# The recurrent heads of a two-block transformer: reordered engine queues, and the masked copy ahead of the operands' update at each level

## What is computed

```
def hgrn2_mixer(q_raw, f_raw, i_in, g_raw, lb, onorm_w):
    """S_t = diag(f_t) S_{t-1} + (1 - f_t) outer i_t ; o_t = S_t^T q_t ; chunkwise."""
    ...
    o = o * lax.rsqrt(jnp.mean(o * o, axis=-1, keepdims=True) + EPS)
    o = o * onorm_w.astype(f32).reshape(HG_HEADS, HG_DV)
    o = o.reshape(bsz, L, HG_WIDTH) * jax.nn.silu(g_raw.astype(f32))

def conv_module(u, cv_w, cv_b, ln_w, ln_b):
    """GLU -> causal depthwise conv over positions -> LayerNorm over channels -> swish."""
    ...
        o_a = hgrn2_mixer(hq, hf, hi, hg, lower_bounds[l], hg_onorm_w[l])
        o_b = dsa_mixer(sq, sk, sv, iq, ik, iw)
        o_c = conv_module(cu, cv_w[l], cv_b[l], cv_ln_w[l], cv_ln_b[l])
        mix = jnp.concatenate([o_a, o_b, o_c], axis=-1) @ w_out[l]
        x = x + g1 * mix
```

## Time and profile before

| | |
|---|---|
| median of 3 runs | 1258.82 us (1256.19 to 1261.29) |
| profiled execution: its time, its span | 1258.17 us, 1256.4 us |
| TensorE busy | 1204.6 us, 96% of the span |
| VectorE, ScalarE, GpSimd busy | 803.6, 689.9, 430.2 us |
| TensorE's granted clock, mean | 0.986 |
| windows of the heads, about | 698 to 866 us from the span's start |

### The profile page before, as it was taken

One profiled execution on the slowest core, in us unless ns is written; L12 is line 12 of the kernel. 1 busy time (PEld: TensorE's weight loads), 2 busy tenths in 40 slices (PEclk: granted clock), 3 DMA queues, 4 the chain that ended last, 5 costly groups with the idle time before them and its releaser, 6 DMA issues. The chain is left out here.

```text
span 1256.4 us, 19744 instructions
## 1 busy us (share of the span) xinstructions
PE 1204.6 (96%) x7198; PEld 976.2 (78%) x7198; DVE 803.6 (64%) x1695; ACT 689.9 (55%) x1337; POOL 430.2 (34%) x260
## 2 busy tenths in 40 slices
PE   9999999997999999999999898788899999999998
PEld 8777777775887777788676676566888889889897
DVE  6776667774577677665798666565763257365575
ACT  6766666674346776735667776533432254353443
...
DMA packets 37983, 127.62 MB, mean 102 GB/s; under 512 B 4592, under 2 KB 7280, under 8 KB 37888
## 3 DMA queue, kind: packets, MB, share of 16 engines
...
q10 hardware_dynamic: 2528, 4.98, 1.2%
...
## 5 line engine op out<-in xcount | busy, mean ns | idle before, releaser
L612 POOL TENSOR_TENSOR wL<-w,wH 128x1024 fp32r<-128x1024 f32 x89 | 222.6, 2505 | 721.6 <-ACT wH L2252 721.4
L1047 PE MATMUL G<-hi,wH 128*128 128x512 f32 x1032 | 421.0, 408 | 13.6 <-DVE xT L1142 9.5
L1049 PE MATMUL G<-hi,wL 128*128 128x512 f32 x1032 | 405.6, 393 | 0.0
L1048 PE MATMUL G<-lo,wH 128*128 128x512 f32 x1032 | 405.5, 393 | 0.0
L1047 PEld LDWEIGHTS G<-hi,wH 128*128 128x128 f32 x1032 | 195.5, 189 | 64.0 <-issue 20.3
L1049 PEld LDWEIGHTS G<-hi,wL 128*128 128x128 f32 x1032 | 195.4, 189 | 43.0
L1048 PEld LDWEIGHTS G<-lo,wH 128*128 128x128 f32 x1032 | 195.8, 190 | 38.9 <-issue 1.9
L2252 ACT ACTIVATE wH<-w 128x1024 fp32r<-128x1024 f32 x140 | 147.5, 1055 | 110.2 <-PE G L1049 59.6
L2805 DVE TENSOR_TENSOR wL<-w,wH 128x1024 fp32r<-128x1024 f32 x51 | 62.2, 1221 | 11.1 <-ACT wH L2252 10.3
L1164 DVE CUSTOM_DVE_ANT_0 adaw<-adaw,scr 128x1024 f32<-128x1024 f32 x36 | 62.9, 1747 | 0.0
L1202 ACT ACTIVATE scr<-scr,sa 128x256 f32<-128x256 f32 (+2 forms) x64 | 35.2, 557 | 23.7 <-DVE sa L1189 23.7
...
## 6 DMA issues: line engine op xcount, KB each, us to landing
...
```

The lines of the kernel that those rows point to most:

```text
L612: g.tensor_tensor(wL[:, u.slot], raw_home(u), wH[:, u.slot].bitcast(f32), ALU.subtract).then_inc(w_lo, 1)
L1047: mm(home[:, :], whi, H[:, k, :], start=(k == first), stop=False)
L1048: mm(home[:, :], whi, L[:, k, :], start=False, stop=False)
L1049: last = mm(home[:, :], wlo, H[:, k, :], start=False, stop=(k == final))
```

## The change

Nothing is computed otherwise. `level_of` runs `joined` and then `raise_both`, where it was the other way about. On VectorE `clamped` and `powers` move from the end of a window and from behind `queries_1` to the window's start, and `silu_vector_2` behind `raise_q`; the norm of the head before stands behind level 3 in place of level 2, its gate behind level 4 and its low part behind level 5; the logistic steps stand later too. On ScalarE the terms, splits and logistic steps are in another order; window 1 takes eight pairs of terms and window 2 three. TensorE begins head 1's first unit before window 0, and in the last window fewer tiles stand ahead of `outputs(3)` and more behind it. Four of the blocks of the modulation go from `add_output` to the end of the last head on VectorE, and their loads move ahead in SyncE's queue.

```diff
-CONV_HEAD = [4, 7, 4, 0]
+CONV_HEAD = [4, 8, 3, 0]
...
-ADA_PER = {"a": (ADA_OA, (0, 1, 1, 1, 1, 0, 0, 0), 32), "b": (ADA_OB, (0, 1, 1, 1, 1, 2), 32), "m": (ADA_OM, (0, 1, 1, 1, 1, 2), 48)}
+ADA_PER = {"a": (ADA_OA, (0, 0, 0, 1, 1, 1, 1, 0), 32), "b": (ADA_OB, (0, 1, 1, 1, 1, 2), 32), "m": (ADA_OM + 4, (0, 0, 0, 1, 1, 0), 48)}
...
-            for n in range(4):
+            for n in range(5):
                 load_unit(Unit(UOM + 1 + n))
-            for n in range(8):
+            for b in range(2, 6):
+                load_ada(Block(ADA_OM, b))
+            for n in range(1, 8):
                 load_unit(Unit(UOM + 5 + n))
-                if 1 <= n <= 4:
-                    load_ada(Block(ADA_OM, n + 1))
             load_ada(Block(ADA_M, 0))
...
+            conv_terms(0, 0)
+            split_h(4)
+            conv_terms(0, 1)
+            conv_terms(0, 2)
+            conv_terms(0, 3)
+            split_h(5)
+            for t in range(1, 4):
+                split_h(4 * t + 2)
+                for slot in range(6):
+                    conv_terms(t, slot)
+                split_h(4 * t + 3)
                 split_h(4 * t + 4)
-                conv_terms(t, 4 if t else 3)
+                conv_terms(t, 6)
+                conv_terms(t, 7)
                 if t < 3:
                     split_h(4 * t + 5)
-                conv_terms(t, 5)
-                conv_terms(t, 6)
...
-            v.memset(stat[:, b.buffer, 0, 0:1], 0.0)
+            v.memset(stat[:, b.buffer, 1, 0:1], 0.0)
...
+                gemm_h(1, 0, (2,))
                 product(0, 0)
                 product(0, 1)
-                gemm_h(1, 0, (0, 1))
+                gemm_h(1, 0, (3, 4))
                 product(0, 2)
                 turn_h(0)
-                gemm_h(1, 0, (2, 3, 4))
+                gemm_h(1, 0, (5,))
                 product(0, 3)
-                gemm_h(1, 0, (5, 6, 7))
+                gemm_h(1, 0, (6, 7))
                 product(0, 4)
...
                 sum_h(t - 1)
+
+            def window(t):
+
+                opened(t)
                 fill(t, 3)
                 product(t, 3)
-
-            def window(t):
-
...
+                if t == 2:
+                    conv_sum()
                 fill(t, 4)
...
-                    conv_sum()
                 fill(t, 5)
                 product(t, 5)
...
                 fill(t, 6)
                 product(t, 6)
-                if t == 2:
-                    conv_sqsum()
                 fill(t, 7, (0, 1))
                 product(t, 7)
...
                 opened(3)
+                fill(3, 3, (0, 1))
+                product(3, 3)
+                fill(3, 3, (2, 3))
+                product(3, 4)
                 output_m(0, (4, 5))
-                output_m(0, (0,))
-                product(3, 4)
-                output_m(0, (1,))
+                product(3, 5)
                 output_m(1, (4, 5))
-                product(3, 5)
+                product(3, 6)
+                output_m(0, (0, 1))
+                product(3, 7)
                 output_m(1, (0, 1))
-                output_m(0, (6,))
-                product(3, 6)
-                output_m(0, (7,))
+                turn_ke(3)
+                output_m(0, (6, 7))
+                updates(3)
                 output_m(1, (6, 7))
-                product(3, 7)
-                output_m(2, (4, 5, 6))
-                turn_ke(3)
-                output_m(2, (7, 0))
-                output_m(0, (2,))
-                updates(3)
-                output_m(1, (2,))
-                output_m(2, (1,))
                 outputs(3)
-                output_m(2, (2,))
-                output_m(3, (4, 5))
+                output_m(2, (4, 5))
                 sum_h(3)
-                output_m(3, (6, 7, 0, 1, 2))
+                for n in range(2):
+                    output_m(n, (2,))
+                output_m(2, (6, 7, 0, 1, 2))
+                output_m(3, (4, 5, 6, 7, 0, 1, 2))
...
             turn_c(pe, 4)
-            gemm_h(0, 3, SECOND)
+            gemm_h(0, 3, (4, 5))
             mix_c(pe, 4)
+            gemm_h(0, 3, (6,))
             turn_c(pe, 5)
+            gemm_h(0, 3, (7,))
+            gemm_h(1, 0, (0,))
             mix_c(pe, 5)
+            gemm_h(1, 0, (1,))
             spread_c(pe, 0)
...
+                terms(CONV_C[5], CONV_C[6])
+                take_hv(0)
+                gate_1(0)
                 conv_terms(0, 0)
-                take_hv(0)
-                conv_terms(0, 1)
-                gate_1(0)
-                conv_terms(0, 2)
                 split_h(4)
                 forget(1)
                 silu_scalar_2(act, "h", 0, zsig)
-                conv_terms(0, 3)
+                conv_terms(0, 1)
+                conv_terms(0, 2)
                 keys(1)
                 factor(1)
+                take_first(0)
+                conv_terms(0, 3)
                 split_h(5)
-                take_first(0)
...
             def window(t):
-                queries(t)
+                raw_h(t, 1, qraw, sem("h_q"), t + since("h_q"))
                 take_ke(t - 1)
+                act.wait_ge(sem("h_raw1"), t + 1 + since("h_raw1"))
+                silu_scalar_1(act, link, "hq", t, qraw[:, :], kraw[:, :])
+                split_h(4 * t + 2)
+                silu_scalar_2(act, "hq", t, kraw[:, :])
                 conv_terms(t, 0)
-                silu_scalar_2(act, "hq", t, kraw[:, :])
-                split_h(4 * t + 2)
                 raw_h(t, 2, vraw, sem("h_vturn"), t + since("h_vturn"))
+                if t == 3:
+                    for k in range(2):
+                        act.wait_ge(sem("conv_z"), k + 1)
+                        silu_scalar_1(act, link, "cv", k, cacc[:, k, :], cv_th[k])
                 conv_terms(t, 1)
+                square_h(t - 1)
+                conv_terms(t, 2)
                 if t == 3:
                     for k in range(2):
                         silu_scalar_2(act, "cv", k, cv_th[k])
-                square_h(t - 1)
-                split_h(4 * t + 3)
-                conv_terms(t, 2)
-                take_hv(t)
-                root_h(t - 1)
-                if t == 3:
                     for k in range(2):
                         act.wait_ge(sem("cv_gated"), k + 1)
                         s.activation(hi1[:, 6 + k, :], cv_th[k], ACT.Copy).then_inc(sem("cv_gated_hi"), 1)
                 conv_terms(t, 3)
+                take_hv(t)
+                root_h(t - 1)
+                conv_terms(t, 4)
                 raw_h(t, 3, zraw, sem("h_silu"), t + since("h_silu"))
-                split_h(4 * t + 4)
                 gate_1(t)
-                conv_terms(t, 4)
-                gated_h(t - 1)
-                if t < 3:
-                    split_h(4 * t + 5)
+                conv_terms(t, 5)
+                split_h(4 * t + 3)
                 if t == 2:
                     for k in range(2):
                         act.wait_ge(sem("conv_centred"), k + 1)
                         s.activation(csq[:, k, :], cacc[:, k, :], ACT.Square).then_inc(sem("conv_sq"), 1)
-                conv_terms(t, 5)
+                gated_h(t - 1)
+                if t < 3:
+                    forget(t + 1)
+                    split_h(4 * t + 4)
                 silu_scalar_2(act, "h", t, zsig)
                 conv_terms(t, 6)
-                if t < 3:
-                    forget(t + 1)
                 if t == 2:
                     act.wait_ge(sem("conv_sqsum"), 1)
                     rsqrt_scalar(link, 1, 1.0 / 256, sem("conv_var"), sem("conv_root"))
                 if t < 3:
                     keys(t + 1)
                     factor(t + 1)
-                if t == 2:
-                    for k in range(2):
-                        act.wait_ge(sem("conv_z"), k + 1)
-                        silu_scalar_1(act, link, "cv", k, cacc[:, k, :], cv_th[k])
                 take_first(t)
+                conv_terms(t, 7)
+                split_h(4 * t + (5 if t < 3 else 4))
 
...
             def level_of(t, n):
+                joined(t, n)
                 raise_both(t, n)
-                joined(t, n)
...
+                level_of(0, 2)
                 low_c(dve, 0)
-                level_of(0, 2)
+                level_of(0, 3)
                 low_c(dve, 1)
-                level_of(0, 3)
                 level_of(0, 4)
+                level_of(0, 5)
                 silu_vector_1(dve, "h", 0, zraw[:, :], zsig)
                 gates(1)
-                level_of(0, 5)
                 level_of(0, 6)
-                clamped(1)
                 raise_both(0, 7)
+            def conv_root():
+                dve.wait_ge(sem("conv_root"), 1)
+                rsqrt_vector(link, 1)
+
+            def conv_scaled(k):
+                w0, b1 = VEC["cv_ln_w_2"], VEC["cv_ln_b_2"]
+                link(v.scalar_tensor_tensor(out=cacc[:, k, :], in0=cacc[:, k, :], scalar=vecT[:, w0 + k:w0 + k + 1],
```

(44 more changed lines are left out.)

30 lines of the change are left out of this document (8 added, 22 removed).

## The result

| | before | changed |
|---|---|---|
| median | 1259.99 us (1256.19 to 1261.29) | 1215.11 us (1214.12 to 1215.96, 4 runs) |
| ratio, 95% interval | 1 | 0.9648 (0.9624 to 0.9673) |
| profiled execution: time, span | 1258.17, 1256.4 us | 1215.79, 1214.0 us |
| mean granted clock | 0.986 | 0.997 |

The account below looks back on a forecast made before the run. TensorE, busy 96% of the span, was taken as the bound, so only its waits and slow stretches could be won: 22.9 + 6.0 − 0.5 − 2.0 = 26.4 us off 1258.2, so 1232 us, range 1223 to 1245.

Parts of the forecast that it names:

- the idle time that this change can reach: TensorE's waits before window 0, in windows 0 to 3 and two behind window 3: 31.3 us in sum.
- the floor of 38.8 us: Most that could be won: 31.3 us of TensorE's idle time plus 7.5 us of slow clock, with no matmul taken away.
- the price of the slow stretches: TensorE's lower clock around five waits, estimated at 1.5 us each, 7.5 in all; four were to go, saving 6.0.
- The waits of the heads: TensorE's waits left before window 0, in windows 0 to 3 and the tail: 8.4 us of 31.3, so 22.9 saved.
- half of one: VectorE operations with two SBUF inputs beside GpSimd: half the 1.2 us stretch counted, giving window 1 a 1.0 us wait.
- Window 3's mechanism: Product 5 waits 3.0 us for level 4, behind ScalarE's root and the norm, with only two tiles per level.
- The tail's two waits: Behind window 3, 3.6 us each for the last head's low part and for rms: both go, 0.5 left.
- the 2.0 kept back: 2.0 us taken off the gain for waits missed in a count by tenths and for a second slow stretch.
- the 0.5 for short pieces: An estimated 0.5 us taken off the gain for more and shorter pieces between TensorE's products.
- the raise becomes the wait: Rival 1: products wait for VectorE's copy, raise and stretched operations, mainly windows 0 and 1; 1240 to 1242 us; chance 0.17.
- The wait did not move into window 3: Rival 2: root, norm and level 4 come later than counted, waits return in window 3; price 15, 1247 us; chance 0.09.
- no load of a block reached TensorE: Rival 4: the load for the block ahead of `states_of(3)` comes late, VectorE and TensorE stand; slower, 1265 us; chance 0.04.

Follow-up runs that it names:

- a_only: The kernel before with only the table of modulation blocks at the first attention's output units changed: 1247.42 us, ratio 0.9899.
- a_back: The changed kernel with only the table of the first output's blocks put back as before: 1226.63 us, ratio 0.9745 to the kernel before.
- norm_back: The changed kernel with the norm of the head before behind level 2 again, not level 3: 1216.28 us, ratio 0.9665 to the kernel before.
- raise_first: The changed kernel with the raise ahead of the masked copy within a level, as before: 1212.44 us, ratio 0.9632 to the kernel before.

## Why the prediction was wrong

**The step that failed** is the first part's "the idle time that this change can reach is 1.7 + 3.9 + 4.9 + 3.3 + 10.3 + 3.6 + 3.6 = 31.3 us", and with it the floor of 38.8 us, "no more": 42.4 were won. The sum has no term for the table of the first output's blocks. It is in the diff, and TensorE's longest wait of the whole span belonged to it. It measured 11.6 us (**a_only**), 11.5 undone (**a_back**). With it the same sum would have given 1220. A second term was too small as well, the price of the slow stretches: 7.5 us for the five that it counted, where the trace shows some 10.2 (below).

**The waits of the heads were right in the sum**, 8.4 us left forecast and 8.5 measured:

| | forecast | measured |
|---|---|---|
| before window 0 | 0.2 | 0 |
| window 0 | 1.8 | 0.91 |
| window 1 | 1.0 | 0.63 + 2.56 |
| window 2 | 1.2 | 0.56 |
| window 3 | 3.7 | 1.90 + 0.33 |
| tail | 0.5 | 1.62 |

The tail is without the 0.2 us that are left of the wait for rms. The idle time by stage above gives nearly the same for the windows: 0, 1.0, 3.3, 0.5 and 2.0 us.

The places are off by up to 2.2 us, and these cancel. Window 1 was dear because its low part waited for a whole split, not half of one; in **norm_back** it began 0.05 us ahead of the split and was not held at all, so what such an operation costs hangs on which of the two starts first. Window 3's mechanism was as forecast: product 5 waits for `raise_both(3, 4)`, behind the norm, behind ScalarE's root. TensorE, and then VectorE, which itself waited 0.22 us for the root:

```profile
802.66 0.96 PE L1878 MATMUL T<-kd 128*64 128x64 f32 x16 [1.90 <-DVE kd L3150]
```

```profile
799.46 0.69 DVE L758 SCALAR_TENSOR_TENSOR sq<-sq,scr 128x512 f32<-128x512 f32 x1 [0.22 <-ACT sq L753]
...
801.92 0.68 DVE L3150 TENSOR_TENSOR kd<-kd,S 128x512 f32<-128x512 f32 x1
```

The tail's two waits went, as said, and another was next: a weight's low part, 1.62 us. The blocks took 1.22 us each there, not 2.1, and the last two waited 3.29 and 1.37 for their loads. The last ended at 823.9, when ScalarE's square of the root had been there for 0.5 us.

```profile
820.00 0.06 DVE L1161 MEMSET stat<- 128x1 f32 x1 [3.29 <-DMA adaw<-ada_dram]
820.04 1.23 DVE L1162 CUSTOM_DVE_ANT_0 adaw<-adaw,scr 128x1024 f32<-128x1024 f32 x1
```

**The slow stretches were sized too small.** Of 42.4 us, 31.3 − 8.5 = 22.8 are waits of the heads and 9.5 − 0.4 = 9.1 those of the table. The rest is 10.5, and TensorE's busy time for the same matmuls fell by 11.0. I estimate each stretch from its trace: the busy time of each half microsecond times the share of the clock that was missing. Before there are six: 2.7 us behind the table's wait, and 1.6, 2.0, 1.5, 1.7 and 3.4 in the order of the earlier trace rows. After there are two of 1.7 each, one behind the 2.56 us of window 1 and one, as forecast, behind product 5 of window 3. The page's slices of 30 us and the stages hide them:

```profile
738.00:746.00 8.00, 8.00 (x38) 6.54 (x36) 4.84 (x12) 7.05 (x12) 5.59 (x4) 0.79 0.06 8
...
802.00:811.00 9.00, 8.34 (x62) 6.22 (x62) 6.22 (x14) 1.83 (x3) 2.53 (x1) 0.81 0.20 58
```

The dearest of before is the one behind the wait for rms. The last row ends in the middle of it; this row, of before, has the rest:

```profile
892.00:900.00 8.00, 7.89 (x41) 7.90 (x42) 3.95 (x13) 3.24 (x8) 0.92 (x1) 0.57 0.04 14
```

So of the 16.0 us that were missed, 11.6 are the table. Of the other 4.4, 0.8 are the stretches (10.2 − 3.4 = 6.8 saved, with a second one left, where 6.0 was forecast with one), 2.5 are the 2.0 kept back and the 0.5 for short pieces, and about 1 us is not assigned.

**The rivals.** That the raise becomes the wait did not happen on balance, but it is there: product 7 of window 1, 2.56 us, a little shorter (2.35) in **raise_first**. The wait did not move into window 3, and no load of a block reached TensorE.

**The changes that carry it**: the table 11.6, the four blocks 6.9, `clamped` and `powers` 8.0, five small moves of 1.2 to 2.1 that make 7.8 by the medians and are not clear of the noise one by one (with the 8.0 and two of nothing it is 14.0 together, not 16.4), and 11.3 us in the heads that are not assigned. The masked copy ahead of the update carries none. The prediction named `clamped` and `powers` in one sentence, as 2 us in hand at product 0; their price was at `turn_ke` and `outputs`, some 2.0 us of it by the collision.
